# A two-block transformer kernel: the first input projection in three fp32r products, and the second attention's first scores moved ahead

## What is computed

```python
h = rmsnorm(x, attn_norm[l])
proj = jnp.einsum('bsd,de->bse', h, w_in[l])          # (256 x 1024) @ (1024 x 3592)
mq, mk, mv, gqkv, gz, ga, gb = jnp.split(proj, offsets, axis=-1)
...
gqkv = jax.nn.silu(causal_depthwise_conv(gqkv, conv_w[l]))
gq = l2norm(gq) * GDN_HEAD_DIM ** -0.5 ; gk = l2norm(gk)
```

## Time and profile before

| | |
|---|---|
| median of 3 runs | 846.87 us (843.25 to 847.81) |
| the profiled execution | 844.62 us, its span 842.7 us |
| busy PE | 773.6 us, 92% of the span |
| busy DVE, ACT | 427.7 us (51%), 297.7 us (35%) |
| mean granted TensorE clock | 0.976 |
| DMA | 208.27 MB, 247 GB/s on average |
| first stage, to the end of the second z block | 127.74 us |

### The profile page before, as it was taken

The page is one execution under the profiler, slowest core; times in us unless marked ns, Lnnn a source line. Parts: engine busy times, 40 slices in busy tenths (PEclk is TensorE's granted clock), DMA queues, the critical chain, the costliest instruction groups (busy, mean ns, idle before and its releaser), DMA issues.

```text
span 842.7 us, 13984 instructions
## 1 busy us (share of the span) xinstructions
PE 773.6 (92%) x5655; PEld 545.6 (65%) x5655; DVE 427.7 (51%) x810; ACT 297.7 (35%) x548; POOL 38.8 (5%) x31
## 2 busy tenths in 40 slices
PE   8999998999989987878778899979998999999998
PEld 6885865565575545526426488656655888888886
DVE  1359224645434330221213497587857676657665
ACT  2134213431134321321303465366642443334331
POOL 1000011001000000000000021300010000000000
PEclk9989998999999999999989799999999999999999
DMA  9862329896989999999999997510005474456301
GB/s 335 289 237 99 137 100 344 307 338 254 401 320 403 402 408 404 404 409 404 404 409 404 401 265 250 179 72 2 1 1 175 146 257 172 150 199 235 115 1 51
DMA packets 124349, 208.27 MB, mean 247 GB/s; under 512 B 7909, under 2 KB 43014, under 8 KB 124174
## 3 DMA queue, kind: packets, MB, share of 16 engines
q1 hardware_dynamic: 123374, 205.39, 66.7%
q10 hardware_dynamic: 864, 2.18, 0.8%
q0 software_dynamic: 64, 0.05, 0.0%
HBM read 206.51 MB, written 1.08 MB: 246 GB/s over the span
## 4 chain that ended last, share of the span: by engine, by line
PE 69%; DMA 10%; SPq 7%; DVE 6%; issue 4%; ACT 3%; POOL 0%; POOLq 0%; DVEq 0%; ACTq 0%
PE psa L581 8%; DMA arena<-in_w_in_dram 6%; PE psv L1231 5%; SPq L413 5%; PE psa L1231 5%; DMA arena<-in_w_down_dram 3%; PE psv L959 3%; PE psa L893 3%; PE psa L833 2%; PE psa L499 2%; PE psv L1232 2%; PE psa L1232 2%; PE psa L501 2%; PE psa L500 2%; PE psv L591 2%
## 5 line engine op out<-in xcount | busy, mean ns | idle before, releaser
L2458 DVE TENSOR_TENSOR unit_parts<-ring,unit_parts 128x2048 fp32r<-128x2048 f32 x33 | 75.5, 2289 | 57.3 <-ACT unit_parts L1810 57.3
L1810 ACT ACTIVATE unit_parts<-ring 128x2048 fp32r<-128x2048 f32 x33 | 62.9, 1912 | 73.9 <-PE psa L1232 43.0
L581 PE MATMUL psa<-arena,ring 128*128 128x256 f32 x320 | 69.9, 380 | 1.0 <-DMA ring<-in_w_in_dram 1.0
L581 PEld LDWEIGHTS psa<-arena,ring 128*128 128x128 f32 x320 | 60.6, 190 | 10.3 <-DVE arena L1868 1.2
L1231 PE MATMUL psv<-column_parts,unit_parts 128*128 128x512 f32 (+1 forms) x192 | 65.5, 389 | 1.6 <-DVE arena L2532 1.4
L1231 PE MATMUL psa<-column_parts,unit_parts 128*128 128x512 f32 (+1 forms) x192 | 65.1, 387 | 0.0
L959 PE MATMUL psv<-ring,arena 128*32 128x256 f32 x976 | 54.9, 380 | 1.4 <-issue 0.7
L1232 PE MATMUL psv<-column_parts,unit_parts 128*128 128x256 f32 (+1 forms) x192 | 52.0, 271 | 0.0
L1232 PE MATMUL psa<-column_parts,unit_parts 128*128 128x256 f32 (+1 forms) x192 | 52.0, 271 | 0.0
L2575 POOL TENSOR_TENSOR small<-small,consts 128x2 f32<-128x2 f32 (+4 forms) x15 | 27.7, 1847 | 474.9 <-DVE small L2313 248.7
L959 PEld LDWEIGHTS psv<-ring,arena 128*32 128x32 f32 x976 | 31.1, 110 | 22.5 <-DMA ring<-in_w_up_dram 2.2
(11 more groups left out here) (408 smaller groups left out, 1505.8 us busy)
## 6 DMA issues: line engine op xcount, KB each, us to landing
ring<-in_w_gate_dram SPq DMA_DIRECT2D x43, 1024.0 KB, 9.4
ring<-in_w_up_dram SPq DMA_DIRECT2D x40, 1024.0 KB, 5.2
arena<-in_w_down_dram SPq DMA_DIRECT2D x32, 1024.0 KB
ring<-in_w_mod_dram SPq DMA_DIRECT2D x24, 1024.0 KB, 7.8
ring<-in_w_in_dram SPq DMA_DIRECT2D x23, 1024.0 KB, 9.3
ring<-in_w_down_dram SPq DMA_DIRECT2D x11, 1024.0 KB, 7.2
ring<-in_w_out_dram SPq DMA_DIRECT2D x8, 1024.0 KB, 7.4
arena<-in_w_in_dram SPq DMA_DIRECT2D x8, 512.0 KB, 12.1
```

The source lines that it names most:

```text
L581: mm = pe.matmul(bank[:, cc * T:(cc + 1) * T], w, hT[:, k, :], start=(k == 0), stop=(k == KD - 1))
L1810: act.activation(unit_parts[q % 3][:, 0, :], slot_of(NPRE + u_), ACT.Copy).then_inc(upper_done, 1)
L2458: vec.tensor_tensor(lo, slot_of(NPRE + at["mlp"] + 3 * n + kind), hi, ALU.subtract).then_inc(lower_done, 1)
```

## The change

**First projection.** The units of `w_in` for `cols_T` and for z now hold 256 columns and all 1024 rows (each still 1 MB, in runs of 1 KB in place of 2 KB); those of the values stay at 512 columns. `cols_T(j)` makes one bank from one unit. The first two units stay fp32. The other 12 are split: ACT copies the rows (`row_parts`) and each unit in fp32r (`upper1`), DVE subtracts (`lower1`), and PE issues three fp32r matmuls for each fp32 matmul. `IN1_FOLLOWS` says which unit's products must be over before a high part's place is written again.

**Second attention.** `scores2(0)` stands right after the turns of "kb". Behind it follow the turns of "qb" and one matmul for the last gate; DVE masks the bias tables in pair 1 and in pair 8, and adds the gate in pair 2.

```diff
-        for c0 in (1536, 2048, 2560):
-            unit512(pre, w_in, c0)
+        for c0 in range(1536, 3072, 256):
+            unit512(pre, w_in, c0, 256)
...
-            unit512(pre, w_in, c0)
+        unit512(pre, w_in, 1024)
+        for c0 in (0, 256, 512, 768, 3072, 3328):
+            unit512(pre, w_in, c0, 256)
+        IN1 = (None, 2, 3, 4, 5, 7, 8, 9, 10, 11, 12, 13, 14)
+        IN1_FOLLOWS = {5: 1, 6: 2, 7: 3, 8: 5, 9: 6, 11: 8, 12: 9}
...
+            def cols_T(j=None):
...
+                for cc in range(2):
+                    for k in range(KD):
...
+                            mm = split_product(o_, [w_[:, k, c_] for w_ in w], [row_parts[:, m, k, :] for m in range(2)],
+                                               k == 0, k == KD - 1)
...
+            def upper1(j):
+                n = IN1[j]
+                act.wait_ge(unit_landed[n % NS], 16 * (n // NS + 1))
+                if j in IN1_FOLLOWS:
+                    act.wait_ge(*at["in1", IN1_FOLLOWS[j]])
+                act.activation(in1_upper[IN1_UPPER[j]][:], slot_of(n), ACT.Copy).then_inc(in1_upper_done, 1)
...
+            def lower1(j):
+                dve.wait_ge(in1_upper_done, j + 1)
+                n = IN1[j]
+                vec.tensor_tensor(ring_lower[:, n % NS, :], slot_of(n), in1_upper[IN1_UPPER[j]][:],
+                                  ALU.subtract).then_inc(in1_lower_done, 1)
...
-            pe.wait_ge(heads_copied, nt)
-            mod_sums(MOD_LAST)
-            pe.wait_ge(v_free, nv)
+            queries_at = nt
             turn_heads("kb", lambda b, cc: pB[:, b, 512 + cc * P:512 + (cc + 1) * P], [0, 1, 2, 3])
-            turn_heads("qb", lambda b, cc: pB[:, b, cc * P:(cc + 1) * P], [0, 1, 2, 3])
...
+            pe.wait_ge(heads_copied, queries_at)
+            pe.wait_ge(a_free, na)
+            scores2(0)
+            turn_heads("qb", lambda b, cc: pB[:, b, cc * P:(cc + 1) * P], [0, 1, 2, 3])
+            pe.wait_ge(mod_copied, MOD_LAST + 1)
+            pe.matmul(PSX[1][:], c("sumrow"), t1, start=True, stop=True).then_inc(last_gate_summed, 1)
...
-            mod_cols(MOD_LAST)
             head_scale("qb", [pB[:, b, 0:512] for b in range(NB)])
-            for b in range(NB):
-                mask_bias(b)
...
                     max2(2 * p)
                     max2(2 * p + 1)
+                    if p in (1, 8):
+                        mask_bias(p // 8)
+                    if p == 2:
+                        last_gate()
```

More of the change, by code:

```diff
@@ L183, in two_blocks @@
         unit_parts = [parts[f"unit_parts{n}"] for n in range(3)]
+        row_parts, in1_upper = parts["row_parts"], [parts[f"in1_upper{n}"] for n in range(5)]
         token_parts, in2_upper = parts["token_parts"], [parts[f"in2_upper{n}"] for n in range(3)]
@@ L573, in _ @@
             pe.wait_ge(a_free, na)
[L574 to L584, removed]
+            def cols_T(j=None):
+                nonlocal nu
+                bank = a_bank()
+                if j is None:
+                    w = unit(1)[0]
+                else:
+                    pe.wait_ge(in1_lower_done, j + 1)
+                    w, nu = in1_views(j), nu + 1
+                for cc in range(2):
+                    for k in range(KD):
+                        o_, c_ = bank[:, cc * T:(cc + 1) * T], slice(cc * P, (cc + 1) * P)
+                        if j is None:
+                            mm = pe.matmul(o_, w[:, k, c_], hT[:, k, :], start=(k == 0), stop=(k == KD - 1))
+                        else:
+                            mm = split_product(o_, [w_[:, k, c_] for w_ in w], [row_parts[:, m, k, :] for m in range(2)],
+                                               k == 0, k == KD - 1)
+                mm.then_inc(a_ready, 1)
+                freed.append((a_ready, na))
+                at["in1", j] = a_ready, na
@@ new lines, in rows_split_nat @@
+            def rows_split_nat(js, take, ready, blocks):
+                nonlocal nu
+                for j in js:
+                    pe.wait_ge(in1_lower_done, j + 1)
+                w = [in1_views(j) for j in js]
+                by_k = w[0][0].shape[1] == 4
+                for b in blocks:
+                    bank = take()
+                    for j in range(2):
+                        for kk in range(w[j][0].shape[1]):
+                            k = 4 * j + kk if by_k else kk
+                            o_ = bank[:] if by_k else bank[:, j * 256:(j + 1) * 256]
+                            mm = split_product(o_, [row_parts[:, m, k, b * P:(b + 1) * P] for m in range(2)],
+                                               [w_[:, kk, :] for w_ in w[j]], k == 0, k == KD - 1)
+                    mm.then_inc(ready, 1)
+                if b == NB - 1:
+                    nu += 2
+                    for j in js:
+                        at["in1", j] = ready, nv if ready is v_ready else na
+                        freed.append(at["in1", j])
@@ L639, in _ @@
             at["sums"] = na
-            rows_nat(unit(2), v_bank, v_ready)
-            cols_T(unit(2))
+            rows_split_nat((5, 6), v_bank, v_ready, range(NB))
+            cols_T(7)
+            cols_T(8)
             pe.wait_ge(log_decay_done, 1)
@@ L680, in _ @@
                 mm.then_inc(v_ready, 1)
-            rows_nat(z_units, a_bank, a_ready, blocks=(1,))
+            rows_split_nat((11, 12), a_bank, a_ready, (1,))
             at["z"] = na
```

105 lines of the change are left out of this document (77 added, 28 removed).

## The result

| | before | changed |
|---|---|---|
| median | 847.34 us (4 runs, 843.25 to 847.86) | 832.53 us (4 runs, 830.56 to 832.58) |
| profiled execution, its span | 844.62, 842.7 us | 832.58, 830.8 us |

A forecast was written before the change was run, and what follows sets the result against it. PE was taken to bound the kernel (92% busy), with DVE becoming the first stage's bound after the change. Terms -8.1 + 0.5 + 0.7 + 0 = -6.9 us gave 837.7 or 838.7, stated as 838.5, range 830 to 844.5.

The forecast's parts named there:

- First stage, -8.1: First projection: the stage ends at 119.6 in place of 127.7 us, with DVE the bound from 40.8 to 103.
- The walk: Instruction-by-instruction timing of the PE, ACT and DVE queues in the changed order, using row durations and 0.1 us per semaphore.
- Packets, +0.5: First stage: units 0 to 4 in 1 KB runs load at 404 in place of 419 GB/s, 0.5 us later.
- Clock, +0.7: First stage: PE's new 4.7 us wait likely brings 6.8 us more half clock; half of 1.4 us taken.
- Second attention, 0: Second attention: the early start is used up by masks, gate and PE's pace; 0 us, bounds -3.2 and +1.9.
- a lead of 3.2 us: Second attention: the first pair's probabilities are ready at 551.2 against 554.4 us.
- the mask in pair 8 eats 1.2 us: Second attention: DVE has no idle time in pair 8, so the second mask of 2.24 us takes the remaining 1.2.
- What PE is spared there comes off the end: First stage: PE alone is the chain, so its savings shorten the kernel as long as ACT and DVE deliver.
- the first rival: Whole kernel: PE stays the bound, DVE and ACT keep up and the attention keeps its lead; 826 us, chance 0.08.
- Slower, charged by packet: First-stage DMA: engines charge by packet, pre[4] lands 12.5 us later; 849.0 us, decides from a landing at 41.3; chance 0.06.
- 15.1 at most: First stage: PE's own saving from split products, 9.9 for cols_T, 2.8 for values, 2.4 for z.

The follow-up runs named there:

- second half alone: Kernel before with only the second attention's new order, first projection as before: 844.17 us, 0.997 of before.
- the mask in halves: Changed kernel with the second attention's second mask in two halves in pairs 5 and 6, in place of pair 8: 832.33 us.
- The last two versions: Changed kernel, first convolution ahead of pre[4]'s parts, second mask halved, PE stream shifted by 102 matmuls: 828.64 us; the same with pre[4] and pre[5] issued early: 828.62 us.
- first half alone: Changed kernel with the second attention in the old order, first projection in split products: 834.63 us, 0.9857 of before.
- shifted by 84: Kernel before with 49 warm-up products of 8 columns in place of 6 of 256 at the start: 842.28 us, 0.9943 of before.
- shifted by 112: Kernel before with 8 of the 13 warm-up products replaced by 64 of 8 columns: 848.57 us, 1.0025 of before.
- `pre[4]` early: Changed kernel with pre[4] and pre[5] issued ahead of the norm rows, sinks, gate rows and router's weights: 828.31 us, 0.9795 of before.
- early convolution: Changed kernel with ACT's second bank of convolution inputs and DVE's first convolution ahead of the parts of pre[4]: 825.34 us, 0.974 of before.

## Why the prediction was right, and where it was not

**First stage, -8.1: right.** The level loop began 8.7 us earlier. The walk's marks stood within 1 us: `pre[4]` at 34.2, convolution from 41.5, a wait ahead of the third sum (3.6 us where 4.7 was said), next to no idle time on DVE to 104. That DVE sets the end of this stage was shown twice: a PE that started 4.7 us late cost 0.3 us, and moving 7.8 us of DVE work into its idle time gave 5.8. The size has some luck in it: the trace of before had 6.8 us of half clock in this stage, and the same program with 3.4 us of it (second half alone) reached the loop at 125.88, which would leave a gain of 6.9.

**Packets, +0.5: not measured by itself.** The unit was taken at 34.2, 0.9 us later than the walk had it without the term and 0.4 later than with it. What share of that the smaller packets have no run tells, and the stage gained more than the walk said even so.

**Clock, +0.7: too much.** The half clock after the small columns was there and grew: windows of the changed kernel.

```profile
52.40:66.10 13.70, 10.12 (x21) 5.00 (x21) 13.03 (x25) 8.93 (x11) 0.00 (x0) 0.50 0.51 166
66.10:68.00 1.90, 1.90 (x10) 1.50 (x8) 1.76 (x5) 1.88 (x2) 0.00 (x0) 1.00 0.00 0
```

It came as feared (13.7 us in place of 6.8). But the run of the mask in halves has the same first stage and only 10.3 us of it, and its level loop began at 118.50, where 13.7 us gave 118.96 and 118.78: 3.4 us of half clock cost 0.3 to 0.5 here. PE has slack there, behind DVE. Where PE is the bound it counts: before, 6.8 us of it gave 127.67, and 3.4 us in the second half alone gave 125.88, 1.8 less for 3.4, half of it, as granted clocks of 0.50 and 1.00 say. The last two versions say the same (1.7 us for 3.4). No run shows the +0.7 by itself: that the new wait brings 6.8 us more of half clock was the author's estimate after the earlier trace rows, and in its place the runs of the changed first stage showed 13.7, 10.3 or 6.8 us of it, with the 0.3 to 0.5 us above as the price of 3.4 us.

**Second attention, 0: right for the profiled pair, too small in general.** First probabilities were ready 19.9 us after the last low part, where the first half alone has 23.1: a lead of 3.2 us, the number forecast. 0.2 to 0.5 us of it reached the end. Where it goes is also as said: a mask of 2.28 us in pair 1, the gate in pair 2, another mask in pair 8. VectorE's timeline:

```profile
541.01 2.28 DVE L2519 TENSOR_TENSOR arena<-arena,consts 128x2048 f32<-128x2048 f32 x1
...
560.72 1.29 DVE L2576 TENSOR_REDUCE small<-psa 128x1 f32<-128x512 f32 x2 [1.02 <-PE psa L1169]
...
570.03 2.28 DVE L2519 TENSOR_TENSOR arena<-arena,consts 128x2048 f32<-128x2048 f32 x1
```

That the mask in pair 8 eats 1.2 us was wrong by 0.8: taken out of there, it gave 0.4. And the walk stood on one trace of before, which had full clock in the whole attention. The other traces of the old order had half clock early in it, and took longer: 94.81 us with 3.4 us of half clock, 96.05 and 96.48 with 6.9 (the kernel before shifted by 84 and by 112). The six traces of the new order with both masks whole took 94.14 to 94.37, with 0 to 6.9 us of half clock. In the old order VectorE waits for PE there (granted clock 0.50 from 561.5 to 563.5 us in the one shifted by 112); the kernel before, and the one shifted by 112 at the same place of its queue:

```profile
562.10 0.69 DVE L2466 TENSOR_REDUCE small<-psa 128x1 f32<-128x512 f32 x1 [0.40 <-PE psv L1122]
```
```profile
567.42 0.69 DVE L2473 TENSOR_REDUCE small<-psa 128x1 f32<-128x512 f32 x1 [2.30 <-PE psv L1129]
```

So the new order is worth 0.2 to 0.5 us where the old one meets little half clock, and 1.7 to 2.3 where it meets 6.9 us of it. This agrees with the medians of the two halves, 1.9 us for the second half alone and 2.1 us between the first half and the whole. The step that failed is the walk at one clock: it had the lead right and left out what the lead is worth when PE slows down. How often a run meets that clock was not counted.

**The missing term.** "What PE is spared there comes off the end" stopped at the end of the first stage. The sum had no term for the work behind it, though every instruction of PE there moved to another place in its stream. Between the level loop and the experts 2.6 us came off: the breaks went from 2.3 to 0.8 us (1.4 us by the sum under the table), and 3.4 us less of half clock goes with the rest. The first part belongs to the places in the stream. The second does not have to: the same program had 3.4, 6.8 and 6.8 us of it in three traces, and none in the one with `pre[4]` early. In the traces the account is 8.7 + 2.65 + 0.5 + 0.25 - 0.2 (the rest took longer) = 11.9, the difference of the spans. The 2.8 us that the medians have more are those by which the profiled execution of before was faster than its median; medians of four runs of a kernel that spreads over 10 us do not say more.

**The level of the forecast.** 838.5 started from the mean of the known runs, 845.6. Later medians of before were 846.1 to 846.7, so this start was sound to 1 us. The lower end of the range is called half-way to the first rival, but half-way from 838.5 to 826 is 832.3; the result, 832.5, lies that close to it. So the mechanism of the first stage held, but the forecast of the time was 6 us too high. In the traces 5.1 us are missing from the sum: 1.8 in the first stage (1.2 of clock and packets that were not paid, 0.6 of the walk), 2.6 between the level loop and the experts, 0.5 behind them, for which no cause was found, and 0.2 in the attention.

**The rivals.** "PE stays the bound", 826, did not come, by the idle times above. The early convolution came near it, at 825.3: there PE waits for next to nothing in the first stage (0.2 us), which is 14.5 us shorter than before, of 15.1 at most. "Slower, charged by packet" fell with the landing at 34.2, far from the 41.3 at which it decided.

## What to carry to other kernels

When a change removes or adds many instructions on an engine, look in the trace of before for idle times whose releaser is "issue" in dense groups of short instructions: here they sat at places of the stream some 125 matmul records with their weight loads apart, and edits ahead of them, of 26 to 112 records, moved them. (Idle times of 0.56 us with the same releaser at the start of L980 in the expert loop stood at that instruction wherever they came: the releaser alone does not tell.) Run the change with one or two fillings off the critical path before crediting a few microseconds to it; here 26 records more at the start cost 3.4 us by the medians, and 102 more gained 2.4. Set the traces side by side by stage with the time at half clock beside each, before a difference of 1 to 3 us is given to an edit: three traces of one program differed by 2.1 us in a stretch of 113. And when a split moves work from TensorE to two other engines, walk their queues first: the idle stretch ahead of the late unit, once filled, gave 5.8 us more.

## What the runs showed of the hardware

- PE stopped for 1.0 to 2.3 us, all but once in dense groups of 64x64 matmuls, with no releaser, at places that moved with the number of instructions ahead (from behind the 43rd of a group to behind the 59th for 112 records more). In the eleven of the fourteen traces that have breaks in this stretch they are the same places counted from PE's first record (722, 846, 974, 1098, 1223, 1348, within 2), and at one of them one trace had 1.67 us and another of the same program nothing. In the kernel before, a packet of 0.02 MB on the instruction queue q8 moves as PE stops (137 to 138 us), and PE went on about 2 us later, at 139.81. The page has 34 such packets in 0.56 MB.
- Half clock costs little where another engine sets the pace (13.7 us of it in the first stage against 10.3: 0.3 to 0.5 us), and half its length where PE does (3.4 us less of it, 1.8 us gained). How much of it a run has is not fixed by the program: 3.4, 6.8 and 6.8 us between the level loop and the experts in three traces of the same instructions.
- The old order of the second attention took 94.60 us at full clock and 96.05 to 96.48 with 6.9 us of half clock; the new order 94.14 to 94.37 with either.
- An fp32r product of 128x256 was 281 to 285 ns in its record with a start every 0.12 us, in the first projection too: records overlap, so the starts give the price, not the mean.
- The small filling matmuls of 8 columns took 3.58 us for 64 records at the start of one run and 2.13 us for 52 in another. Where they were slow, the turns behind them were too, at a granted clock that the profile gives as 1.00 (4 to 16 us), and the first product came 4 us late. What decides between the two was not found.
